# Attention in a two-layer decoder trunk: units of two heads side by side, with the mask as the first product into each score bank

## What is computed

```python
# C: 64 of width, keys in blocks of 256: for 512 tokens the blocks
#    selected plus the own one are all earlier positions
s_own = einsum('bhqd,bhkd->bhqk', qc, k_own) * scale
s_own = where(kpos[None, :] <= qpos[:, None], s_own, NEG)
...
# D: 64 of width plus a rotary part of 32 that the heads' keys share
sc = (einsum('bhqd,bhkd->bhqk', qn, k_nope) + einsum('bhqd,bkd->bhqk', qr, k_rope)) * scale
sc = where(kpos[None, :] <= qpos[:, None], sc, NEG)
p = softmax(sc, axis=-1)
return einsum('bhqk,bhkd->bhqd', p, v)
```

## Time and profile before

| | |
|---|---|
| median of 3 runs | 1233.34 us (1233.25 to 1234.29) |
| profiled execution, its own time | 1234.61 us |
| profiled execution, its span | 1232.8 us |
| TensorE busy | 1196.1 us, 97% |
| VectorE busy | 815.6 us, 66% |
| ScalarE busy | 581.5 us, 47% |
| GpSimd busy | 204.6 us, 17% |

### The profile page before, as it was taken

How to read it: one execution, slowest core, us unless ns; L and a number is a source line. 1 busy time by engine, 2 the same in 40 slices (tenths; PEclk the granted TensorE clock), 3 DMA queues, 4 the chain that set the end, 5 groups by cost and what they waited for, 6 DMA issues and landing times.

```text
span 1232.8 us, 15490 instructions
## 1 busy us (share of the span) xinstructions
PE 1196.1 (97%) x6004; PEld 1005.9 (82%) x6004; DVE 815.6 (66%) x1160; ACT 581.5 (47%) x883; POOL 204.6 (17%) x190
## 2 busy tenths in 40 slices
PE   6999998999999999999999999999999999999997
PEld 6887877888888888888888877878888888888886
DVE  4699767578666666544758887657766666664454
ACT  4455466545444444434545645756444444443442
POOL 1275155110000000000005732612000000000000
PEclk9999999999999999999999999999999999999999
DMA  8233322534333333466633324135333333326573
GB/s 246 73 85 85 90 44 99 166 112 120 101 88 103 92 96 103 155 195 214 193 97 90 87 82 101 68 108 160 94 103 103 97 92 103 92 96 200 175 224 134
DMA packets 155035, 146.84 MB, mean 119 GB/s; under 512 B 4783, under 2 KB 135763, under 8 KB 154963
## 3 DMA queue, kind: packets, MB, share of 16 engines
q1 hardware_dynamic: 154384, 145.12, 39.0%
q10 hardware_dynamic: 579, 0.74, 0.2%
HBM read 139.54 MB, written 2.10 MB: 115 GB/s over the span
## 4 chain that ended last, share of the span: by engine, by line
PE 79%; DVE 10%; POOL 4%; issue 3%; ACT 2%; DMA 1%; POOLq 0%; DVEq 0%; ACTq 0%
PE ps L523 26%; PE ps L525 25%; PE ps L524 25%; DVE wsp L425 2%; POOL rms_r L878 1%; POOL cf_out L887 1%; DVE ps L1157 1%; PE ps L774 1%; PE ps L799 1%; DVE yt L958 1%; PE ps L585 1%; POOL prob L904 1%; ACT wsp L417 1%; DVE rot L1034 1%; POOL wsp L425 1%
## 5 line engine op out<-in xcount | busy, mean ns | idle before, releaser
L523 PE MATMUL ps<-xn,wsp 128*128 128x512 f32 (+1 forms) x1120 | 412.7, 368 | 8.6 <-DVE xn L978 8.6
L425 DVE TENSOR_TENSOR wsp<-raw,wsp 128x1024 fp32r<-128x1024 f32 (+2 forms) x250 | 307.2, 1231 | 160.3 <-ACT wsp L417 160.1
L524 PE MATMUL ps<-xn,wsp 128*128 128x512 f32 (+1 forms) x1120 | 409.9, 366 | 0.0
L525 PE MATMUL ps<-xn,wsp 128*128 128x512 f32 (+1 forms) x1120 | 409.8, 366 | 0.0
L417 ACT ACTIVATE wsp<-raw 128x1024 fp32r<-128x1024 f32 (+2 forms) x256 | 266.1, 1041 | 167.7 <-PE ps L525 128.6
L523 PEld LDWEIGHTS ps<-xn,wsp 128*128 128x128 f32 x1120 | 212.6, 190 | 43.8 <-DVE xn L978 9.9
L525 PEld LDWEIGHTS ps<-xn,wsp 128*128 128x128 f32 x1120 | 212.5, 190 | 34.0
L524 PEld LDWEIGHTS ps<-xn,wsp 128*128 128x128 f32 x1120 | 212.6, 190 | 33.9 <-issue 0.5
L523 PE MATMUL ps<-wsp,hid 128*128 128x512 f32 (+1 forms) x488 | 189.9, 389 | 0.4 <-DVE wsp L425 0.4
L525 PE MATMUL ps<-wsp,hid 128*128 128x512 f32 (+1 forms) x488 | 189.1, 387 | 0.0
L524 PE MATMUL ps<-wsp,hid 128*128 128x512 f32 (+1 forms) x488 | 189.0, 387 | 0.0
(11 more groups left out here) (150 smaller groups left out, 1302.8 us busy)
## 6 DMA issues: line engine op xcount, KB each, us to landing
raw<-in_w_ffn_up SPq DMA_DIRECT2D x88, 512.0 KB, 3.8
raw<-in_w_ffn_down SPq DMA_DIRECT2D x88, 512.0 KB, 4.2
raw<-in_w_in SPq DMA_DIRECT2D x36, 512.0 KB, 3.9
raw<-in_w_out SPq DMA_DIRECT2D x32, 512.0 KB, 3.4
x<-in_x SPq DMA_DIRECT2D x4, 512.0 KB, 8.3
xn<-xn SPq DMA_DIRECT2D x8, 256.0 KB, 3.3
out_x<-x SPq DMA_DIRECT2D x4, 512.0 KB, 4.1
raw<-in_w_vkr SPq DMA_DIRECT2D x4, 432.0 KB, 3.7
```

Source lines behind the costliest of these rows:

```text
L425: eng.tensor_tensor(wsp[:, u % SPLIT, 1, 0:nk * n], raw[:, (l * NU + u) % RAW, 0:nk * n], fp(wsp[:, u % SPLIT, 0, 0:nk * n]), ALU.subtract ...
L523: pe.matmul(dst, a[0], b[0], start=start, stop=False, skip_group_check=True)
L524: pe.matmul(dst, a[0], b[1], start=False, stop=False, skip_group_check=True)
L525: return pe.matmul(dst, a[1], b[0], start=False, stop=stop, skip_group_check=True)
```

## The change

- **Units of two heads.** A step is now a unit: one head's chunks 0 and 1 together, or its chunk 2, or its chunk 3 (`PARTS`). Two heads are a pair, and a pair's six units go head, head, part by part: 24 steps and not 32. `scores` is called on even steps and writes both heads' units.
- **Products alternate.** In group C the products of the two heads, on rows 0 to 63 and 64 to 127, are written alternately, into two banks (L812). Score banks are four and not two, and a bank is free when its exponential is done.
- **Mask.** `mask` writes -1e30 above the diagonal into the bank as the first product, identity times mask (L781, L785); the scores add to it. The scale is put on the keys. VectorE then only takes the maximum, and the exponential reads the bank; `sm` is gone.
- **Values.** The pair's second head uses 128 stationary columns, then the first head 64, which write over the lower half of the same bank. So one copy empties two heads.
- **Clock keepers** stand before the transposes of the first 12 units, and twice in the first three steps; they use the transposes' bank.
- **Output rows 0 and 1** stand inside the attention loop, behind the last two transposes (`OUT_EARLY`).
- **Weights.** GpSimd's three low parts are made in halves, behind units 9, 10, 12, 13, 15 and 16; ScalarE's high parts at 8, 11 and 14. There are five `prob` buffers.

The diff, cut to its core:

```diff
-STAT, SCORE0, PT_BANKS = 4, 5, (2, 3)
+STAT, SCORE_BANKS, PT_BANKS = 4, (5, 6, 7, 4), (2, 3)
...
-PV_BANKS = (0, 1, 7)
+PV_BANKS = (0, 1)
...
-N_ATT = 2 * HEADS * TC
-NPROB = 3
...
+PARTS = ((0, 1), (2,), (3,))
+PAIRS = HEADS
+STEPS = 2 * len(PARTS)
+N_UNIT = PAIRS * STEPS
+N_ROW = 2 * HEADS * TC
+NPROB = 5
 TRAIL = 3
-VALUES_AFTER = (3, 5, 6)
+VALUES_AT = (3, 7, 8)
+PV_TAKEN = 9
 ATT_TAIL = TRAIL + 5
+OUT_HI, OUT_LO = (8, 11, 14), (9, 10, 12, 13, 15, 16)
+OUT_EARLY = {N_UNIT + 1: 0, N_UNIT + 2: 1}
+
+
+def unit(t):
+
+    pair, r = divmod(t, STEPS)
+    return pair, r // 2, r % 2
...
+def chunks_of(t):
+
+    pair, part, i = unit(t)
+    return [(slice((c == 1) * P, ((c == 1) + c + 1) * P), (2 * pair + i) * TC + c) for c in PARTS[part]]
+
+
+def blocks_of(t):
+    return sum(c + 1 for c in PARTS[unit(t)[1]])
...
-        sm = place("sm", [P, 2, T], f32, tmp_at + 10240)
...
+                PRODUCTS = ((0, 0), (0, 1), (1, 0))
+
+                def mask(t):
+
+                    bank, part = SCORE_BANKS[t % 4], unit(t)[1]
+                    if part == 0:
+                        pe.matmul(ps[:, bank, :].rearrange("p (c k) -> p c k", c=2)[:, :, 0:P], ident_r[:, :],
+                                  causal_r[:, :].unsqueeze(1).broadcast_to([P, 2, P]), start=True, stop=False,
+                                  skip_group_check=True)
+                    else:
+                        pe.matmul(ps[:, bank, (part + 1) * P:(part + 2) * P], ident_r[:, :], causal_r[:, :],
+                                  start=True, stop=False, skip_group_check=True)
+
                 def scores(t):
-                    h, c = divmod(t, TC)
-                    if t < 2:
-                        bank_free(l, (G_MK, G_MV)[t])
+
+                    pair, part, _ = unit(t)
...
-                        pe.wait_ge(masked, l * N_ATT + t - 1)
...
+                        pe.wait_ge(exp_done, l * N_UNIT + t - 2)
...
+                    if pair < PAIRS // 2:
+                        q, k = hid[:, QM + pair], hid[:, KM + pair]
+                        for i in range(2):
+                            mask(t + i)
+                        for c, (cols, _) in chunks:
+                            for a, b in PRODUCTS:
+                                for i in range(2):
+                                    r = slice(DH * i, DH * i + DH)
+                                    last = pe.matmul(ps[:, SCORE_BANKS[(t + i) % 4], cols], q[r, a, c * P:(c + 1) * P],
+                                                     k[r, b, 0:(c + 1) * P], start=False, stop=a == 1, skip_group_check=True)
+                                    if a and c == PARTS[part][-1]:
+                                        last.then_inc(score_done, 1)
                     else:
-                        if c == 0:
-                            if t == N_ATT // 2:
-                                pe.wait_ge(keys_moved, (l + 1) * 32)
-                                pe.wait_ge(queries_moved, (l + 1) * 32)
-                                pe.wait_ge(kr_placed, (l + 1) * 64)
-                                pe.wait_ge(rope_placed, (l + 1) * 64)
-                        q, k = ml_q[h - HEADS], ml_k[h - HEADS]
                         r = slice(0, MLA_QK)
-                    n = (c + 1) * P
-                    product(ps[:, SCORE0 + t % 2, 0:n], (q[r, 0, c * P:n], q[r, 1, c * P:n]),
-                            (k[r, 0, 0:n], k[r, 1, 0:n]), True, True).then_inc(score_done, 1)
+                        for i in range(2):
+                            h = 2 * (pair - PAIRS // 2) + i
+                            q, k = ml_q[h], ml_k[h]
+                            mask(t + i)
+                            for c, (cols, _) in chunks:
+                                last = product(ps[:, SCORE_BANKS[(t + i) % 4], cols],
+                                               (q[r, 0, c * P:(c + 1) * P], q[r, 1, c * P:(c + 1) * P]),
+                                               (k[r, 0, 0:(c + 1) * P], k[r, 1, 0:(c + 1) * P]), False, True)
+                            last.then_inc(score_done, 1)
...
+                def keep_clock(bank):
+
+                    pe.matmul(ps[:, bank, :], ident_r[:, :], vm[:, 0, 0:2, :].rearrange("p c d -> p (c d)"),
+                              start=True, stop=True, skip_group_check=True)
 
                 def transposes(t):
-                    c = t % TC
-                    pe.wait_ge(prob_done, l * N_ATT + t + 1)
+                    bank = PT_BANKS[t % 2]
                     if t >= 2:
-                        pe.wait_ge(pt_ready, l * N_ATT + t - 1)
...
+                        pe.wait_ge(pt_ready, l * N_UNIT + t - 1)
...
+                    if t < N_UNIT // 2:
+                        keep_clock(bank)
+                    pe.wait_ge(prob_done, l * N_UNIT + t + 1)
+                    for b in range(blocks_of(t)):
+                        last = pe.transpose(ps[:, bank, b * P:(b + 1) * P], prob[:, t % NPROB, b * P:(b + 1) * P],
+                                            ident[:, :])
                     last.then_inc(pt_done, 1)
...
+                def values(pair, part):
+
+                    g = G_PV + pair
                     if part < 2:
-                        pe.wait_ge(pt_ready, l * N_ATT + TC * h + (TC if late else 2))
+                        pe.wait_ge(pt_ready, l * N_UNIT + STEPS * pair + (2, STEPS)[part])
...
+                    v = vm if pair < PAIRS // 2 else vl
+                    c0 = pair % 2 * P
+                    for i in ((1, 0), (1,), (0,))[part]:
+                        m = P if i else DH
+                        for kc in range(4 if part else 2):
+                            skip = P if kc == (3 if part else 1) else 0
+                            out_cols = slice((part > 0) * 2 * P + skip, ((part > 0) * 2 + 2) * P)
+                            probs = [pt_late[:, i, s, kc, skip:2 * P] if part else pt_early[:, i, s, 2 * kc * P:(2 + kc) * P]
+                                     for s in range(2)]
+                            last = product(ps[0:m, bank_of(g), out_cols], [v[:, s, kc, c0:c0 + m] for s in range(2)], probs,
+                                           kc == 0, skip > 0)
+                    if part == 0:
+                        last.then_inc(pv_early, 1)
                     if part == 2:
                         last.then_inc(group_done, 1)
...
+                def out_row(half, k):
+                    if half == 0 and k == 0:
+                        pe.wait_ge(y_ready, l * 4 + 4)
+                        pe.wait_ge(exp_done, (l + 1) * N_UNIT)
...
+                    row_product(l, U_OUT + half * KD + k, k, KD, MIX, half)
...
+                for t in range(N_UNIT + ATT_TAIL):
+                    if t < N_UNIT and t % 2 == 0:
                         scores(t)
-                    for _ in range(2 if t < TRAIL else 1 if t < N_ATT // 2 else 0):
-                        keep_clock()
-                    if TRAIL <= t < N_ATT + TRAIL:
+                    if t < TRAIL:
+                        if t == 0:
+                            bank_free(l, G_MK + 1)
+                        for _ in range(2):
+                            keep_clock(PT_BANKS[1])
+                    for hp in range(PAIRS):
+                        if t - TRAIL - STEPS * hp in VALUES_AT:
+                            values(hp, VALUES_AT.index(t - TRAIL - STEPS * hp))
+                    if TRAIL <= t < N_UNIT + TRAIL:
                         transposes(t - TRAIL)
...
+                    if t in OUT_EARLY:
+                        out_row(0, OUT_EARLY[t])
...
+                for t in range(N_UNIT):
+                    pool.wait_ge(inv_done, l * N_UNIT + t + 1)
+                    for cols, row in chunks_of(t):
+                        last = pool.tensor_tensor(prob[:, t % NPROB, cols], prob[:, t % NPROB, cols],
+                                                  rowinv[:, row:row + 1].to_broadcast([P, cols.stop - cols.start]), ALU.mult)
+                    last.then_inc(prob_done, 1)
...
-                    if t in (15, 19, 23):
-                        u = U_OUT + (t - 15) // 4
-                        pool.wait_ge(lo_done, l * NU + u)
-                        split_lo(pool, l, u)
+                    if t in OUT_LO:
+                        i, part = divmod(OUT_LO.index(t), 2)
...
+                        out_lo_part(i, part)
...
-                        dve.tensor_tensor_reduce(out=sm[:, t % 2, 0:n], in0=ps[:, SCORE0 + t % 2, 0:n],
-                                                 in1=causal[:, T - n:T],
-                                                 scale=-(MOBA_SCALE if t < N_ATT // 2 else MLA_SCALE), scalar=3e38,
-                                                 op0=ALU.add, op1=ALU.min, accum_out=negmax[:, t:t + 1])\
-                           .then_inc(masked, 1)
...
+                    if t < N_UNIT:
+                        dve.wait_ge(score_done, l * N_UNIT + t + 1)
+                        for cols, row in chunks_of(t):
```

(21 more changed lines are left out.)

210 lines of the change are left out of this document (97 added, 113 removed).

## The result

The changed kernel takes **1220.08 us** (median of 4, 1218.60 to 1221.48) against 1233.30 for the kernel before in the same comparison: ratio 0.9891, 95% interval 0.9874 to 0.9908. The forecast was 1226.7 with a range of 1221 to 1233: the sign was right, the change is 13.2 us where 6.6 was forecast, and the time lies just under the range. The profiled execution after took 1219.48 us, with a span of 1217.7.

The account below looks back on a forecast made before the run. TensorE, busy for 97% of the span, was taken as the bound. Attention terms summed to -3.3 us a layer, -6.6 for two, from the median 1233.34 to 1226.7 us; range 1221 to 1233.

Parts of the forecast that it names:

- Side by side: Group C score products of two heads run at the same time: -3.8 us a layer, bounds 0 and -3.8.
- loads take turns: Rival: group C products overlap but weight loads do not, gaining 1.9 us for 3.8; 1229.5 us, chance 0.27.
- no overlap: Rival: alternating group C products run one by one; -0.9 us a layer, 1231.5 us, chance 0.20.
- Fewer entries: Sixteen 64-row score sets become six; ten entries fewer at 0.21 us each: -2.1 us a layer.
- 64-column values: Half of the value products get 64 stationary columns; narrower loads and crossings together +0.3 us a layer.
- lower bound of -1.4: 24 narrow value products a layer fall from 0.12 to 0.06 us with the shorter weight load.
- upper +1.7: Eight 64-column value stretches a layer each entered and left at 0.21 us, the price of a 64-row set.
- the rival of the emptied array: Value products' width changes, 16 a layer, make the array run empty: +1.2 us a layer, 1235.7 us, chance 0.08.
- Masks: One mask product ahead of each of 24 attention units at 0.12 us: +2.9 us a layer, upper bound +4.1.
- Waits: TensorE's waits in the attention stage go from 3.0 to 2.7 us a layer: -0.3, bounds -2.7 and +1.5.

Follow-up runs that it names:

- apart: Changed kernel with the other head's mask, a product over all rows, standing between the two heads' 64-row products in group C; 1229.33 us, ratio 0.9966.
- wide: Changed kernel with 128 stationary columns in all value products, the second head's values being overwritten; 1222.98 us, ratio 0.9920.
- b_first: Kernel before the change with each step's value products ahead of its transposes, not behind them; 1235.52 us, ratio 1.0022.
- late_rows: Changed kernel with output rows 0 and 1 behind the attention loop, as before the change; 1226.68 us, ratio 0.9942.
- nokeep: Changed kernel without its 18 clock keepers a layer; 1219.62 us, ratio 0.9886.

## Why the prediction was wrong

*Where the time is.* Right: all of it lies in the attention stage and on TensorE. The forecast for the stage was 58.3 us, measured 54.1.

*Where the sum went wrong.* The table above charges each product with the time to the next start, so the costs of seams (the places where one kind of product gives way to another) lie scattered over its rows. Sorted by cause, with each product at the spacing that it has among its own kind and the rest put to the seams (us a layer, worked out from the same timelines):

| | before | after | change | forecast |
|---|---|---|---|---|
| group C scores at their own price | 7.4 | 3.7 | -3.7 | -3.8 |
| 64-row sets, 16 and 6, entered and left | 6.4 | 2.7 | **-3.7** | **-2.1** |
| masks at their own price | - | 1.9 | **+1.9** | **+2.9** |
| values at their own price | 15.8 | 14.9 | **-0.9** | **+0.3** |
| clock keepers at their own price | 4.4 | 4.2 | -0.2 | -0.3 |
| named waits | 3.0 | 2.4 | -0.6 | -0.3 |
| all the rest | 24.7 | 24.3 | -0.4 | 0 |
| stage | 61.7 | 54.1 | -7.6 | -3.3 |

Three terms make 3.8 of the 4.3 us by which the forecast was short.

*Side by side: right.* -3.7 for -3.8, and the choice between the bounds was right: apart against the changed kernel shows factor two. The Trainium skill's sentence on row groups ("TensorE: Matmul & The Clock Gate", Part 3) agrees with the trace. The rivals "loads take turns" and "no overlap" fall: 12 products of 128 and 256 columns take 0.89 us (161.02 to 161.91), 0.15 a pair, where turns would need 0.24.

*Fewer entries: the step that failed most.* "Ten entries fewer at 0.21" was read inside the set, 0.72 - 0.51, and left out its neighbours. The product ahead of a set and the one behind it pay 0.10 each as well, which stands in the earlier trace rows: a set costs 0.40, and ten fewer bring 3.7. The term for entries and overlap together looked right (-5.5 for -5.9 in the scores' own row), because the missing part stands in other rows: keepers, values and transposes.

*64-column values: the wrong sign.* "+0.3" was the sum of two guesses. The width is worth -1.1 on the values' row in both directions of test and 1.05 of stage in wide, near the lower bound of -1.4. The spacing alone gives -0.9: eight times three products of 128 moving columns take 0.18 in place of 0.28. No crossing costs anything, so the upper +1.7 and the rival of the emptied array fall. Of the Trainium skill's drain on a change of tiling mode ("TensorEngine Tiling (Array Packing)", Key Properties) nothing is seen between 128 and 64 columns; whether the array changes its mode there no run shows. Between 128 and 64 rows a set costs the 0.40 above.

The values' row falls by 3.5 and not by 0.9 to 1.1. Most of the rest isn't theirs. Before, 22 separate runs of value products follow transposes, and 4 after: 18 x 0.08 = 1.5 that other rows take over, as b_first shows. Seven runs led into a 64-row set before and none does after: 7 x 0.09 = 0.7, part of the sets' price. The last 0.4 are mostly short delays ahead of transposes.

*Masks.* Priced at 0.12 each, they cost 0.06 (16 of 128 columns) and 0.12 (8 of 256) at their own spacing, 1.9 in all. Their row shows +3.5, 0.15 each, because six of them lead into a 64-row set (0.8) and ten stand first behind transposes (0.8, which the transposes give back). Group D's scores lose 1.0 where 0 was put: 0.9 of it are delays of 0.12 to 0.17 us ahead of transposes, too short for the waits view, which are gone; what caused them wasn't traced.

*Waits.* The sum was right (2.4 measured, 2.7 forecast), the cause half wrong: three waits of four are for VectorE's low part, which two transposed banks allow only two units ahead, and the piece for output row 3 is 0.16 us at 209.91. The price of the tail was underrated: the prediction gave the early rows credit for the 0.8 us that the kernel before waits there. In the changed kernel the rows in their late place would cost 4.3 a layer (late_rows), because the waits there are longer and the clock falls.

*Gain and median.* Of the 15.2 us in the stages some 1.5 come back outside them, which leaves 13.7, near the 13.2 of the medians; of the 1.5 output row 3's waits are 0.3, the rest wasn't traced. The clock stayed full in both stages, as forecast.

## What to carry to other kernels

Price an order by its seams, not only by its products, and read a seam on both sides: the last product ahead of it, and the first behind it. Here the set of 64-row products cost 0.21 us inside and as much again on its neighbours. Then check the opposite error: a product that looks dear behind another kind may only take back what its neighbour gave way early, so add the two before calling it a cost. Two half-row products overlap fully as soon as nothing over all rows stands between them; strict alternation isn't needed, one product over all rows between them undoes it. Work moved into a wait may be worth more than the wait, since a longer one can lower the clock for what follows, in some executions and not in others; ask of each filler whether it does more than fill a wait.

## What the runs showed that was not expected

- Disjoint row halves overlap even if three products of one head come ahead of three of the other (5.05 against 5.00 us).
- A shorter product doesn't pass its saving on: 16-bit masks lose 1.6 us of their own cost and the stage 0.2.
- The products behind transposes look 0.08 us dearer and the last transpose 0.08 cheaper, at every such place: moving work from behind the transposes saved nothing.
- Merging stretches of value products made the kernel before slower (1.0031) although the values themselves fell by 1.2 us a layer.
- Waits of 0.6 and 1.65 us at the end of attention were followed by a granted clock of 0.66 over 5 us, one of 2.0 us at its start by 0.81 in that ten-microsecond window; nokeep, with 6.3 us of waits, kept it full in its profiled stage.
